# Scores by row halves, and a dense network on raw turned tokens with the norm as a row at the gate

## The reference

```python
def rms_norm_2(x, gain):
    xf = x.astype(jnp.float32)
    y = xf * lax.rsqrt(jnp.mean(xf * xf, axis=-1, keepdims=True) + EPS)
    return (y * gain.astype(jnp.float32)).astype(x.dtype)

def swiglu(x, w_gate, w_up, w_down):                 # D_MODEL 1024, D_FF 3584
    return (jax.nn.silu(x @ w_gate) * (x @ w_up)) @ w_down

# each attention, per block of 128 queries (heads of 64 channels; 32 in the differential one)
s = jnp.einsum('bhqd,bhkd->bhqk', q, k) * scale      # masked but in the first layer
p = jax.nn.softmax(s, axis=-1)
o = jnp.einsum('bhqk,bhkd->bqhd', p, v)

# layer 0 of the second block
c = rms_norm_2(h, norm_ffn[0])
h = h + swiglu(c, ffn_w_gate[0], ffn_w_up[0], ffn_w_down[0])
gate = jax.nn.sigmoid(rms_norm_2(h, ple_norm[0]) @ ple_w_gate[0])
h = h + (p[0] @ ple_w_proj[0]) * gate
```

## Time and profile before

| what | us |
|---|---|
| median of 3 runs (2447.03 to 2450.59) | 2447.05 |
| the profiled execution | 2447.15 |
| its span | 2445.4 |
| TensorE busy in the span | 2250.2 |
| VectorE busy | 1854.6 |
| ScalarE busy | 1529.0 |
| GpSimd busy | 50.4 |
| mean granted clock of TensorE | 0.954 of full |

### The profile page before, as it was taken

One profiled execution on the slowest core, in us unless ns is written; L12 is line 12 of the kernel. 1 busy time (PEld: TensorE's weight loads), 2 busy tenths in 40 slices (PEclk: granted clock), 3 DMA queues, 4 the chain that ended last, 5 costly groups with the idle time before them and its releaser, 6 DMA issues. The chain is left out here.

```text
span 2445.4 us, 36780 instructions
## 1 busy us (share of the span) xinstructions
PE 2250.2 (92%) x11988; PEld 1849.2 (76%) x11988; DVE 1854.6 (76%) x2058; ACT 1529.0 (63%) x1995; POOL 50.4 (2%) x61
## 2 busy tenths in 40 slices
PE   7988699998987799979987799999999999999997
PEld 6777577776765699977765678888888888888885
DVE  4655698885766555546767599999999999999995
ACT  4554398885633444436533377777777777777774
POOL 0000000000002100000003000000000000000000
PEclk9989899999987899999977899999999999999998
DMA  8434199996620266645610299999999999999991
GB/s 295 146 114 127 65 387 363 339 355 235 180 91 1 79 195 195 188 130 168 189 32 6 79 357 349 362 350 358 353 354 357 349 362 344 375 333 377 333 377 57
DMA packets 280617, 593.69 MB, mean 243 GB/s; under 512 B 26272, under 2 KB 39488, under 8 KB 280384
## 3 DMA queue, kind: packets, MB, share of 16 engines
q1 hardware_dynamic: 280512, 592.32, 68.4%
HBM read 591.19 MB, written 1.05 MB: 242 GB/s over the span
## 5 line engine op out<-in xcount | busy, mean ns | idle before, releaser
L416 DVE TENSOR_TENSOR ring_lo<-ring,ring_hi 128x1024 fp32r<-128x1024 f32 (+1 forms) x1120 | 1337.2, 1216 | 287.7 <-ACT ring_hi L411 230.3
L411 ACT ACTIVATE ring_hi<-ring 128x1024 fp32r<-128x1024 f32 (+1 forms) x1120 | 1161.4, 1054 | 460.2 <-PE psum L434 407.1
L432 PE MATMUL psum<-ring_hi,xg_hi 128*128 128x512 f32 x896 | 355.3, 397 | 5.9 <-PEq L189 3.5
L434 PE MATMUL psum<-ring_hi,xg_lo 128*128 128x512 f32 x896 | 350.5, 391 | 0.0
L433 PE MATMUL psum<-ring_lo,xg_hi 128*128 128x512 f32 x896 | 349.9, 390 | 0.0
L432 PE MATMUL psum<-ring_hi,xT_hi 128*128 128x512 f32 (+2 forms) x512 | 202.1, 395 | 17.9 <-DVE ring_lo L416 11.2
L432 PEld LDWEIGHTS psum<-ring_hi,xg_hi 128*128 128x128 f32 x896 | 168.9, 188 | 39.9 <-issue 3.7
L433 PE MATMUL psum<-ring_lo,xT_hi 128*128 128x512 f32 (+2 forms) x512 | 198.3, 387 | 0.0
L434 PE MATMUL psum<-ring_hi,xT_lo 128*128 128x512 f32 (+2 forms) x512 | 197.9, 386 | 0.0
L434 PEld LDWEIGHTS psum<-ring_hi,xg_lo 128*128 128x128 f32 x896 | 168.8, 188 | 36.0
L433 PEld LDWEIGHTS psum<-ring_lo,xg_hi 128*128 128x128 f32 x896 | 169.1, 189 | 33.8
(11 more groups left out here) (517 smaller groups left out, 3213.4 us busy)
## 6 DMA issues: line engine op xcount, KB each, us to landing
ring<-in_moe_w_gate_dram SPq DMA_DIRECT2D x224, 512.0 KB, 5.4
ring<-in_moe_w_up_dram SPq DMA_DIRECT2D x224, 512.0 KB, 5.4
ring<-in_moe_w_down_dram SPq DMA_DIRECT2D x224, 512.0 KB, 4.9
ring<-in_w_in_dram SPq DMA_DIRECT2D x76, 512.0 KB, 5.1
ring<-in_w_gate_dram SPq DMA_DIRECT2D x64, 512.0 KB, 5.0
ring<-in_w_up_dram SPq DMA_DIRECT2D x64, 512.0 KB, 5.5
ring<-in_w_down_dram SPq DMA_DIRECT2D x64, 512.0 KB, 5.4
ring<-in_ffn_w_gate_dram SPq DMA_DIRECT2D x28, 512.0 KB, 4.4
```

Source lines behind the costliest of these rows:

```text
L411: sc.activation(raw_view(ring_hi, FINE, num, a, width), raw_view(ring, RAW, num, a, width), ACT.Copy) \
L416: v.tensor_tensor(raw_view(ring_lo, FINE, num, a, width), raw_view(ring, RAW, num, a, width), raw_view(ring_hi, FINE, num, a, width).bitca ...
L432: pe.matmul(out_, lhsT[0], rhs[0], start=start, stop=False)
L434: return pe.matmul(out_, lhsT[1], rhs[0], start=False, stop=stop)
```

## The change

In `attend`, keys lie packed, both heads' rows full, and each head is scored by a product on its own 64 rows; the two row halves write to two banks (`c` in `s_[:, c, a:b, :]`). So the heads stand in another order in the accumulators (`slots`). The zeroed blocks of the first layer and of the sparse attention go; the differential one keeps a half as large block, since its heads have 32 channels. Cross attention keeps its products and has its two heads in two banks.

The dense network no longer has `normed_T` ahead. A class `Lead` carries its parts into `dense_experts`: the raw x is transposed and gets the gain, as before, but no norm. The norm is made beside the first gate pieces (`scalar_row`), laid out as a row over tokens by two small products (`tensor_row`), and multiplied onto the gate's accumulators on VectorE ahead of Silu, which then reads `s_g`. The up part needs no norm, since the output is multiplied by it per token when it is added to x (`combine` is `rinv`). The last step's hidden values have a tile of their own, `last_hiddenT`, the last two steps' downs are summed in the accumulators, and the sum is added to x once, by halves, each as soon as it is done. The next stage's splits come ahead of that.

```diff
             def views(m):
@@
-                s_ = psum[:, (m % 2) * 2 * BANK:(m % 2) * 2 * BANK + n * k].rearrange("p (h k) -> p h k", h=n)
+                s_ = bank(m % 2 * 2, 2).rearrange("p (c x) -> p c x", c=2)[:, :, 0:n // 2 * k].rearrange("p c (n k) -> p c n k", k=k)
@@
-                        for qT, kT, a, b in j["scores"]:
-                            last = pe.matmul(s_[:, a:b, :], qT, kT, start=True, stop=True)
+                        for qT, kT, c, a, b in j["scores"]:
+                            last = pe.matmul(s_[:, c, a:b, :], qT, kT, start=True, stop=True)
@@ def tensor(e) of dense_experts
+                if lead:
+                    lead.tensor(e)
@@
                                 if part == 0 and q == 0 and prev:
-                                    e.wait_ge(silu.sem, i + silu.at(0))
+                                    free = scaled if lead else silu
+                                    e.wait_ge(free.sem, i + free.at(0))
@@
+                            if lead and part == 0 and not prev:
+                                lead.tensor_row(e)
                     if prev:
                         e.wait_ge(hid.sem, i + hid.at(0))
-                        if not (isinstance(i, int) and i == 1):
+                        if not (isinstance(i, int) and i == 1 or lead and final):
                             e.wait_ge(y_out.sem, i + y_out.at(-1))
+                        before_last = lead and isinstance(i, int) and i == group.steps - 1
+                        h_now = last_hidden if final else (h_hi, h_lo)
@@
-                                                        [w_[:, 0, c * BANK:(c + 1) * BANK] for w_ in w], j == 0, j == 3)
+                                                        [w_[:, 0, c * BANK:(c + 1) * BANK] for w_ in w],
+                                                        j == 0 and not (lead and final), j == 3 and not before_last)
+                                if lead and final and j == 3 and h == 0:
+                                    half_done.inc(last)
@@ def scalar(e)
-                        sc.activation(h_hi[:], s_g[:], ACT.Copy).then_inc(hid_hi.sem, 1)
+                        sc.activation((h_hi if cur else last_hidden[0])[:], s_g[:], ACT.Copy).then_inc(hid_hi.sem, 1)
@@
+                        if lead:
+                            e.wait_ge(scaled.sem, (1 if isinstance(i, int) and i == 0 else i + 1) + scaled.at(0))
+                            sc.activation(flat_g, flat_g, ACT.Silu).then_inc(silu.sem, 1)
@@ def vector(e)
                     if prev:
-                        e.wait_ge(used, count_after(group.number(0 if cur else 8, i, cur), 0))
+                        if lead and not cur:
+                            e.wait_ge(used, count_after(group.number(7, group.steps - 1)))
+                        else:
+                            e.wait_ge(used, count_after(group.number(0 if cur else 8, i, cur), 0))
@@
+                    if lead and done == 0:
+                        add_outputs(0, ((half_done.sem, half_done.at(1)), (used, count_after(group.number(11, group.steps, None)))))
@@
+                            v.tensor_tensor(s_g[:], G.rearrange("p (j n) -> p j n", j=4), row_bc(lead.row[:], [4]), ALU.mult) \
+                                .then_inc(scaled.sem, 1)
@@
+    class Lead:
...
+        def tensor(self, e):
+            for b in range(4):
+                for m in range(4):
+                    k, h = 2 * b + m // 2, m % 2
+                    last = pe.transpose(bank(4 + b)[:, m * P:(m + 1) * P], x[:, h, k * P:(k + 1) * P], ident)
+                self.turned_x.inc(last)
+            e.wait_ge(self.x_lo.sem, self.x_lo.at(4))
+
+        def tensor_row(self, e):
+
+            e.wait_ge(self.diag_ok.sem, self.diag_ok.at(1))
+            for h in range(HALVES):
+                last = pe.matmul(bank(4)[:, h * P:(h + 1) * P], const("all_ones"), self.diag[:, h, :], start=True, stop=True)
+            self.row_done.inc(last)
...
+        def scalar_row(self, e):
+            for h in range(HALVES):
+                self.sq.inc(sc.activation(self.junk[:, h, :], x[:, h, :], ACT.Square, accum_out=self.ss[:, h:h + 1]))
+            e.wait_ge(self.sq.sem, self.sq.at(HALVES))
+            self.act.inc(sc.activation(self.rms[:], self.ss[:], ACT.Ln, scale=1.0 / D, bias=eps))
+            e.wait_ge(self.act.sem, self.act.total)
+            self.rms_done.inc(sc.activation(self.rinv[:], self.rms[:], ACT.Exp, scale=-0.5))
+            use_table(SILU)
...
@@ the sparse attention's jobs
-                    jobs.append(dict(scores=[(q, kpad[:, keys, :, 0:n], 2 * m, 2 * m + 2) for m, q in enumerate(qs)],
+                    jobs.append(dict(scores=[(qT[ch, m, tok], kT[ch, keys, 0:n], c, m, m + 1) for m in range(MH // 2) for c, ch in head_rows],
@@ the first layer's attention
-            attend([dict(scores=[(qT[:, 2 * g + n, h * P:(h + 1) * P], kpad[:, g, :, :], 2 * n, 2 * n + 2) for n in range(2)],
+            attend([dict(scores=[(qT[ch, 2 * g + n, h * P:(h + 1) * P], kT[ch, g, :], c, n, n + 1) for n in range(2) for c, ch in head_rows],
@@ layer 0
-            normed_T(x, g_ffn2[layer], xT, xn)
-            all_tokens_experts(lambda h, ex: const("all_ones")[:, 0:1])
+            all_tokens_experts(g_ffn2[layer])
```

More of the change, by code:

```diff
@@ L568, in idle, with product @@
             yield
-    def product(lhsT, kt, cols, copy_to=None, add_to=None, loads=(), table=None, beside=None, banks=8, clear=None):
+    def product(lhsT, kt, cols, copy_to=None, add_to=None, loads=(), table=None, beside=None, banks=8):
         def steps(n, e):
@@ L734, in _ @@
                         use_table(LOG_EXP)
+    head_rows = [(c, slice(c * HD, (c + 1) * HD)) for c in range(2)]
     def attend(jobs):
@@ L820, in shift @@
                         mx = small[m % 2][0][:, 0:j["nh"]]
+                        pair = [2, j["nh"] // 2]
                         e.wait_ge(scores.sem, scores.at(m + 1))
                         if "mask" in j:
-                            part = s_[:, :, j["keys"] - j["mask"].shape[-1]:]
-                            step(v.tensor_tensor(part, part, row_bc(j["mask"], [j["nh"]]), ALU.add))
-                        step(v.tensor_reduce(mx, s_, AXX, ALU.max))
+                            part = s_[:, :, :, j["keys"] - j["mask"].shape[-1]:]
+                            step(v.tensor_tensor(part, part, row_bc(j["mask"], pair), ALU.add))
+                        step(v.tensor_reduce(mx.rearrange("p (c n) -> p c n", c=2), s_, AXX, ALU.max))
                         step(v.tensor_scalar(mx, mx, -j["scale"], None, ALU.mult), max_ready)
@@ L869, in exp @@
                         e.wait_ge(max_ready.sem, max_ready.at(m + 1))
-                        for h in range(jobs[m]["nh"]):
-                            last = sc.activation(E[:, h, :], s_[:, h, :], ACT.Exp, bias=mx[:, h:h + 1],
+                        half = jobs[m]["nh"] // 2
+                        for i, h in enumerate(jobs[m].get("slots", range(2 * half))):
+                            last = sc.activation(E[:, h, :], s_[:, i // half, i % half, :], ACT.Exp, bias=mx[:, i:i + 1],
                                                  scale=jobs[m]["scale"], accum_out=rs[:, h:h + 1])
@@ L892, in dense_experts @@
             "silu_ready", "hidden_made", "hidden_hi_ready", "hidden_ready", "expert_output_added"))
[L893 removed]
+        scaled, half_done = (lead.scaled, lead.half_done) if lead else (None, None)
+        counted = (silu, hidden, hid_hi, hid)
         def programs(st):
@@ L897, in programs @@
             h_hi, h_lo = tmp_split(st, "hiddenT", [P, 4, SEQ])
+            last_hidden = tmp_split(st, "last_hiddenT", [P, 4, SEQ]) if lead else (h_hi, h_lo)
             flat_g = s_g[:].rearrange("p j n -> p (j n)")
             def tensor(e):
+                if lead:
+                    lead.tensor(e)
                 def body(i, cur, prev, done):
+                    final = prev and not cur
                     if cur:
@@ L977, in body @@
                         e.wait_ge(hid_hi.sem, i + hid_hi.at(0))
-                        v.tensor_tensor(h_lo[:], s_g[:], h_hi[:].bitcast(F32), ALU.subtract).then_inc(hid.sem, 1)
-                    if one and ((prev and not prev[2]) or done == 0):
+                        hi, lo = (h_hi, h_lo) if cur else last_hidden
+                        v.tensor_tensor(lo[:], s_g[:], hi[:].bitcast(F32), ALU.subtract).then_inc(hid.sem, 1)
+                    if lead and cur and prev and not prev[2]:
                         add_outputs(0)
-                        e.wait_ge(y_out.sem, group.steps + y_out.at(0) if i is None else i + y_out.at(-1))
+                        e.wait_ge(y_out.sem, i + y_out.at(-1))
+                    if lead and done == 0:
+                        add_outputs(0, ((half_done.sem, half_done.at(1)), (used, count_after(group.number(11, group.steps, None)))))
+                        e.wait_ge(y_out.sem, group.steps - 1 + y_out.at(0))
                     if cur:
@@ L987, in body @@
```

(8 more changed lines are left out.)

135 lines of the change are left out of this document (88 added, 47 removed).

## The result

The changed kernel took 2429.45 us (median of 7 runs, 2421.54 to 2435.75), beside 2447.03 us for the kernel before (7 runs, 2445.50 to 2450.59). By the medians it is 17.6 us, 0.72%, faster. The ratio, which goes by the means, is 0.9921, with a 95% interval from 0.9908 to 0.9934: 16 to 23 us. The forecast was 2417 us with a range of 2411 to 2427. The direction was right; the median lies 12.5 us above the forecast and 2.5 above the range. The profiled execution, at 2422.17 us, is one of the short ones.

What follows compares the result with a forecast made beforehand. TensorE was taken to bound the dense network's steady part, chains with no full engine the other places touched. 5.6 + 14.8 + 9.4 + 0.4 = 30.2 us off 2447.15 gave 2417 us, range 2411 to 2427.

Steps and rivals of the forecast that it cites:

- Part 1: Ahead of the dense network: first product 5.1 us earlier, 0.4 lost to the norms' row, 0.9 won by clock; 5.6 us.
- Part 2: Each inner dense step: VectorE's extra product delays Silu and splits some 2.3 us, within 6.2 us to spare; cost 0.
- Part 3: Last inner dense step and stage behind: 7.6 us gap closed, 1.6 clock, 3.6 tail, 2.0 next stage; 14.8 us won.
- Part 4: Attention scores by row halves: two halves run at once, so VectorE waits less for scores; 9.4 us won.
- the rival on the clock: Attention: TensorE does less, granted clock falls by 0.05 over three stages' 130 us, up to 6 us return; 2423, chance 0.10.
- rival D: From the experiments' forecasts: fixed cost per change between row halves and full rows, whatever the clock; halves alone 2449 to 2452 us.
- the signs: Marks named ahead: mask's waits for a score under 0.4 us would show right, granted clock in attention under 0.80 wrong.
- Serial halves: Attention scores: the two row halves don't overlap, 3 us lost instead of 9.4 won; 2429 us, chance 0.08.
- overlap in part: Attention scores: halves overlap partly, five pass times instead of four, 1.07 us a job; 2419.5 us, chance 0.12.
- a down 6 that still waits: End of dense network: down 6 waits for a split or the last hidden, some 7 us stay; 2424, chance 0.08.
- the slower case: Dense steps: splits queue behind Silu, TensorE waits once delay per step passes 6.2 us; slower than before, chance 0.02.
- The 0.4 us of copies: Attention: the compressed keys' copy, of 64 rows, ends a stage; 0.18 us saved twice, 0.4 us won.

Runs made afterwards that it cites:

- dense_alone: Changed kernel with the attention of the kernel before (full-row scores), so only the dense network's change is in; 2424.80 us, 0.9897 of the kernel before.
- late_3: dense_alone with three more unused reductions ahead of the product with the row of norms in each of seven steps; 2426.68 us, 0.9899.
- one_place: dense_alone with the last step's hidden values in the tile of all other steps; 2435.41 us, 0.9938.
- dense_again: dense_alone measured once more, beside the changed kernel on the same chip; 2428.41 us, 0.9915.
- halves_alone: Kernel before with the scores by row halves and nothing else of the change; 2449.13 us, 0.9994.
- after_third: The changed kernel measured again, beside dense_again on the same chip; 2428.93 us, 0.9918.
- first_fill: dense_alone with row halves in the first layer's attention only, plus ten, then two unread transposes ahead of waits for exponentials in three attention stages; 2410.72 us, 0.9845.
- late_8: dense_alone with eight more unused reductions ahead of the product with the row of norms in each of seven steps; 2477.72 us, 1.0107.
- after_again: The changed kernel measured once more, unaltered; 2429.94 us, 0.9924.
- the fill runs: Kernels with extra transposes of a constant, which nothing reads, ahead of TensorE's waits for exponentials in attention; ratios from 0.9845 to 0.9899.
- fill_8: Changed kernel with eight extra unread transposes ahead of each wait for exponentials in attention, cross attention included; 2424.67 us, 0.9899.
- fill_4: Changed kernel with ten extra unread transposes ahead of each attention stage's first wait for exponentials, four ahead of later ones, none in cross attention; 2418.03 us, 0.9881.

## Why the prediction was wrong

**Part 1** held. From x complete to the first product 5.4 us were won, where 5.1 stood; the row of norms cost 0.44 (0.4 stood: in the fine record of TensorE's starts the lead over the kernel before goes from 12.18 to 11.74 us at those two products); the low clock at the start of the stream lasted 2.9 us instead of 3.5, 0.3 won in this execution instead of 0.9, and all of it in others (from the first product to down 0 dense_alone has no low clock and takes 46.62 us for 47.70 before, the row of norms included). In sum 5.2 for 5.6.

**Part 2** held: no cost, and late_3 shows more than 3 us of slack left.

**Part 3** held. Down 6 ends 9.15 us earlier against the stream, for 7.6 + 1.6 forecast, and one_place takes 7.7 us of it back. The tail gave 4.1 for 3.6, the stage behind 2.5 for 2.0. Parts 1 to 3 give 21.0 us between the two traces, for 20.4; the medians of dense_alone and dense_again give 24.4 and 20.8. So of the 12.6 us between 30.2 forecast and 17.6 measured, some 10 are Part 4's, and the rest lies within what one kernel's median moves between chips.

**Part 4** is the step that failed: "9.4 us won" was 0 in the median (halves_alone; after_third against dense_again). Its mechanism held as far as the scores go. The halves run side by side: 16 records in 2.00 us at the full clock. The Trainium skill (TensorE: Matmul & The Clock Gate, Part 3) says that products start and end in strict program order; the records agree as far as starts go, in pairs some 0.01 to 0.04 us apart, but no fifth pass time is lost: that this order costs one was my inference. At equal clock 8.4 us came back, and the waits for scores shrank by 3.9 and 3.3 us for 3.8 and 4.1. What failed is the sentence in the rival on the clock: "If that falls by 0.05 over the three stages' 130 us, up to 6 us come back", with a chance of 0.10. It fell by 0.13, from 0.77 to 0.64 over 138 us: 36 us more at the low level. What a us at that level costs here can be read across the kernels with full rows and no fill: from 60 us low and 137.5 us of attention (one_place) to 73 and 141.6 (late_3), 0.33 each. At that price 36 us cost some 12. The kernels with halves and no fill show a lower one, from 75 us low and 134.8 (halves_alone) to 98 to 99 and 137.2 to 138.9 (the changed kernel's three profiles), about 0.15 each, or 5 us. So the halves' gain at equal low time lies between 5 and 12 us, and what the clock took back is as much; how much it is exactly stays open, and so does the share of rival D's fixed cost. That the two cancel is measured.

Two sources of the error can be named. I took the clock as given by the stage, while it answers to what TensorE does in it: with each score issued twice the low time fell from 99 to 66 us, so the removed half passes were work that had kept the clock up. And the 4.9 and 5.2 us of waits for scores were in part the low clock's work already: first_fill's second mixer has full rows at 0.89 and waits 1.8 us. The same gain could be had through the clock or through the halves, not twice. Two of the signs were set badly as well: the longest wait for a score under a mask was 1.0 us, not under 0.4, and a clock under 0.80 in attention was no sign of a fall, since the kernel before already had 0.78 and 0.73 in its mixers, of which the earlier trace rows shows only part of the first.

**The other rivals.** Serial halves, overlap in part and a down 6 that still waits are ruled out by the rows above; the slower case needs a delay that late_3 does not reach and late_8 does. The 0.4 us of copies can't be told from the clock's shifts in their stages.

**The range** took the profiled executions as the kernel's time. Among six runs and more of one kernel the shortest and the longest mostly differ by 11 to 16 us, the longer ones at a lower clock (the changed kernel 2421.5 at 0.949 and 2435.8 at 0.943), against 3.6 us over the three runs shown before. 2422.17 was inside the range, the median was not, and the first was luck: of the 25.0 us between the two profiled executions 21.0 are Parts 1 to 3, attention lost 0.4, and 4.4 lie in other stages, where the low stretches fell elsewhere. after_again's profiled execution took 7.6 us longer with attention only 0.4 longer, so this scatter is not attention's alone.

## What to carry to other kernels

In a stage whose end is a chain between engines, TensorE's work in its gaps is not waste alone: here it moved the clock at which the links of the chain run. Before taking work from TensorE there, read the granted clock of that window, work out what the time at the low level costs, and count the gain only at the clock that is left. Where the clock was low, a few products that nothing reads, into a bank about to be overwritten, were worth 5 to 10 us of 2430; where it was full anyway (cross attention), eight of them, 0.11 us apart, cost 0.66 us a job. And of a kernel with such stages several runs with their clocks are needed, since single runs differ by more than the halves were forecast to win.

## What the hardware showed beyond expectation

- The clock fell without long idle times. In the second mixer of the changed kernel TensorE was busy 50.6 of 58.5 us by the records, at most 2.9 us idle at a time, and still got 0.54; the kernel before, once idle for 3.5 us, got 0.73. (At the low clock the same work is busy for longer.) The Trainium skill (TensorE: Matmul & The Clock Gate, Part 1) says that "the default state is throttled, and activity releases the throttle"; the fill runs agree, with 99 us at the low level in attention down to 39 by four transposes a job.
- Eight extra transposes a job (fill_8: 36 us low) held the clock no better than four (fill_4: 39), and cost 6 us more in the three stages, 135.3 against 129.3.
- Where the low stretches fall is not the code's alone: in the first layer's attention the same kernel, in two executions on two chips, took 23.4 us with 0.6 us low (dense_again) and 27.3 with 10.2 (dense_alone). What sets this from run to run was not found.
